# Down products of two feed-forwards: the middle eight inner tiles as 2x2 blocks with seven block products

## The reference, cut to what matters

```
x = x + (silu(hn @ w_up[:, :2816]) * (hn @ w_up[:, 2816:])) @ w_down                 # first block
u = causal_dwconv(h @ w_up, conv_w, 3 taps) + conv_b;  gate, val = split(u)           # second block
x = layer_norm(ALPHA * x + (1 + gt_f) * ((silu(gate) * val) @ w_down), g, b)
```

## Time and profile before

| | |
|---|---|
| median of 3 runs | 3579.56 us (3576.22 to 3579.78) |
| the profiled execution | 3572.89 us, span 3571.2 us |
| PE busy | 3412.1 us (96%), 16130 matmuls |
| DVE busy | 1965.6 us (55%) |
| ACT busy | 1356.3 us (38%) |
| POOL busy | 461.3 us (13%) |

### The profile page before, as it was taken

One profiled execution on the slowest core, in us unless ns is written; L12 is line 12 of the kernel. 1 busy time (PEld: TensorE's weight loads), 2 busy tenths in 40 slices (PEclk: granted clock), 3 DMA queues, 4 the chain that ended last, 5 costly groups with the idle time before them and its releaser, 6 DMA issues.

```text
span 3571.2 us, 39536 instructions
## 1 busy us (share of the span) xinstructions
PE 3412.1 (96%) x16130; PEld 2770.9 (78%) x16130; DVE 1965.6 (55%) x2371; ACT 1356.3 (38%) x1880; POOL 461.3 (13%) x325
## 2 busy tenths in 40 slices
PE   7999999999899899999999999999899989999998
PEld 4778887877777578888888877777698768888886
DVE  7454452233554434687773264444576678888335
ACT  3232112333145733433331146353545454444213
POOL 0000000000001000344540010000000035554000
PEclk9999999999999999999999999999999999999999
DMA  3213241112410013233238322120203312333732
GB/s 111 61 38 123 97 165 60 48 48 81 139 51 27 27 51 112 95 112 111 107 122 320 112 83 92 59 100 30 95 1 124 118 71 106 113 112 140 309 105 83
DMA packets 114390, 353.82 MB, mean 99 GB/s; under 512 B 16009, under 2 KB 25993, under 8 KB 114193
## 3 DMA queue, kind: packets, MB, share of 16 engines
q1 hardware_dynamic: 114208, 351.28, 28.1%
HBM read 268.15 MB, written 81.91 MB: 98 GB/s over the span
## 4 chain that ended last, share of the span: by engine, by line
PE 82%; DVE 8%; ACT 7%; issue 1%; DMA 1%; SPq 0%; ACTq 0%; DVEq 0%
PE PS L491 41%; PE PS L2334 21%; PE PS L474 8%; PE PS L3678 1%; PE PS L1817 1%; PE PS L3690 1%; PE PS L2809 1%; ACT whi L431 1%; DVE wlo L436 1%; PE PS L1526 1%; ACT dS L1580 1%; PE PS L503 1%; PE PS L918 1%; PE PS L1839 1%; PE PS L509 1%
## 5 line engine op out<-in xcount | busy, mean ns | idle before, releaser
L436 DVE TENSOR_TENSOR wlo<-raw,whi 128x1024 fp32r<-128x1024 f32 (+3 forms) x393 | 499.1, 1271 | 443.9 <-ACT whi L431 441.3
L431 ACT CAST whi<-raw 128x1024 fp32r<-128x1024 f32 (+3 forms) x393 | 372.4, 948 | 745.4 <-PE PS L491 337.1
L491 PE MATMUL PS<-xhi,whi 128*128 128x512 f32 x1904 | 617.6, 406 | 32.5 <-DVE xlo L525 12.8
L491 PE MATMUL PS<-xlo,whi 128*128 128x512 f32 x1904 | 594.7, 394 | 0.0
L491 PE MATMUL PS<-xhi,wlo 128*128 128x512 f32 x1904 | 592.2, 392 | 0.0
L491 PEld LDWEIGHTS PS<-xhi,whi 128*128 128x128 f32 x1904 | 355.3, 191 | 123.5 <-issue 28.6
L491 PEld LDWEIGHTS PS<-xlo,whi 128*128 128x128 f32 x1904 | 362.2, 190 | 78.0
L491 PEld LDWEIGHTS PS<-xhi,wlo 128*128 128x128 f32 x1904 | 361.5, 190 | 77.8
L2334 PE MATMUL PS<-tf,whi 128*128 128x512 f32 x936 | 288.2, 389 | 1.7 <-DVE wlo L436 1.7
L2334 PE MATMUL PS<-xhi,whi 128*128 128x512 f32 x624 | 243.8, 391 | 7.2 <-DVE xlo L2319 5.6
L2334 PE MATMUL PS<-xlo,whi 128*128 128x512 f32 x624 | 243.5, 390 | 0.0
(11 more groups left out here) (553 smaller groups left out, 5554.2 us busy)
## 6 DMA issues: line engine op xcount, KB each, us to landing
raw<-in_w_up SPq DMA_DIRECT2D x88, 512.0 KB, 3.4
hid<-hs SPq DMA_DIRECT2D x88, 512.0 KB, 3.6
raw<-in_w_in SPq DMA_DIRECT2D x67, 512.0 KB, 3.2
slot<-hid SPq DMA_DIRECT2D x56, 512.0 KB, 6.5
adr<-in_w_ada SPq DMA_DIRECT2D x48, 512.0 KB, 4.5
raw<-in_w_down SPq DMA_DIRECT2D x48, 512.0 KB, 3.5
raw<-in_w_gate SPq DMA_DIRECT2D x32, 512.0 KB, 3.3
merged<-hid SPq DMA_DIRECT2D x16, 512.0 KB, 12.8
```

The source lines that it names most:

```text
L431: act.e.copy(whis[i % RING][:, ks, :], raws[i % RING][:, ks, :]).then_inc(*give("w_hi", i))
L436: dve.e.tensor_tensor(wlos[i % RING][:, ks, :], raws[i % RING][:, ks, :], whis[i % RING][:, ks, :].bitcast(F32), ALU.subtract).then_inc(*g ...
L491: ins = pe.e.matmul(ps[:, h * 512:(h + 1) * 512], w[s][:, k, :], x[:, h * 512:(h + 1) * 512], start=(at == 0 and n == 0), stop=(at == kt - ...
```

## The change

The middle part (hidden tiles 6 to 13) of both feed-forwards is no longer eight products of 8 x 3 x 2 = 48 matmuls (384 in all). Output tiles j and j+4 together, inner tiles {6, 8, 10, 12} against {7, 9, 11, 13}, and the two halves of the tokens form a 2x2 block product with seven block products of 12 matmuls: 4 x 84 = 336 matmuls.

- Weights: the host reorders the inner tiles (`DOWN_ORDER`); POOL makes sums of the weight halves as in the up products; there are `_s12` and `_s34` units in the plan.
- Hidden tiles: four sums of block halves are made beside the up products. In the iteration behind tiles 6, 8, 10, 12 VectorE makes `h1` in place; behind tiles 7, 9, 11, 13 it makes `h2`, `h3` and `h4`, ScalarE casts them (`sums_hi`, `last_hi`) and VectorE makes their `lo` (`h23_lo` over 1024 tokens, `h4_lo` over 512). SP stores them too (`store_sums`).
- Down: seven operand forms (B11, B21, B22, T1 to T4) of 2 MB each are loaded from `hid`, in rows of 2 KB, in place of eight hidden tiles of 1 MB. ScalarE copies two of the seven results, and VectorE adds to the residual in 11 operations of 512 tokens for each j.
- The last part begins with three half products interleaved tile by tile, since hidden tiles 18 to 21 can only be loaded when the last forms are no longer read.

```diff
+        def down_blocks_pe(pe, f):
+            as_banks()
+            def part(unit, at, form, name, read, *signal):
+                pe.wait_ge(f"lane{FORM_LANE[form]}", f, "form", 1)
+                block_product(pe, unit, at, DF[form], (name, f, j), read, *signal)
+            for j in range(4):
...
+                part(a, 0, "B11", "d1", ("dn_p1", f, j), "dn_1", f, j)
+                part(a, 4, "B21", "d2", ("dn_c11", f, j), "prod", a)
+                part(b, 4, "T4", "d4", ("dn_c21", f, j), "prod", b)
+                part(s12, 0, "T1", "d5", ("dn_p5c", f, j), "dn_5", f, j)
+                part(s12, 4, "T2", "d6", ("dn_u2", f, j), "prod", s12)
+                part(s34, 0, "T3", "d7", ("dn_u3", f, j), "dn_7", f, j)
+                part(s34, 4, "B22", "d3", ("f%d_x" % f, 1, j), "prod", s34)
+            as_pairs()
...
+        def other_sums(dve, f, i, u, v):
+            n = SECOND[i]
+            dve.wait_ge(f"f{f}_lo", i - 1)
+            dve.wait_ge(f"f{f}_h", i)
+            dve.e.tensor_tensor(u[:, half[1]], v[:, half[1]], u[:, half[1]], ALU.subtract).then_inc(*give("h2", f, n))
+            dve.wait_ge("h2", f, n)
+            dve.e.tensor_tensor(u[:, half[0]], u[:, half[1]], u[:, half[0]], ALU.subtract).then_inc(*give("h3", f, n))
...
+            for j in range(4):
+                begin_sp(sp, DOWN[f], j, 6)
+                if j == 0:
+                    load_form(sp, f, "T3")
+                    load_form(sp, f, "B22")
+                    load_hidden(sp, f, 14)
+                    load_hidden(sp, f, 15)
...
-            for ft in range(8):
-                down_half(pe, 1, ft, 0, hs)
-            for ft in range(8):
-                down_half(pe, 1, ft, 1, hs)
+            drive([down_half(pe, 1, ft, 0, hs) for ft in range(3)])
+            for ft in range(3, 8):
+                drive([down_half(pe, 1, ft, 0, hs)])
+            for ft in range(8):
+                drive([down_half(pe, 1, ft, 1, hs)])
                 ln0_first_pe(pe, ft)
```

More of the change, by code:

```diff
@@ L142, in weight_plan @@
     ups("w_up", PLAIN[0])
[L143 to L147, removed]
+    downs("w_down")
     tiles("w_in2", [ft for _, ft in PROJ], 8)
@@ L151, in weight_plan @@
     ups("w_up2", PLAIN[1])
[L152 to L157, removed]
+    downs("w_down2")
     return plan
@@ L2269, in ffn_pool @@
+            for i in range(18, 22):
+                load_hidden(sp, f, i)
+            for ft in range(16):
+                begin_sp(sp, DOWN[f], ft % 8, 14)
         def ffn_pool(pool, f):
@@ L2323, in build, with block_product @@
         fast = [6, 7, 0, 1, 2, 3, 4, 5]
+        def block_product(pe, unit, at, x, name, read, *signal):
+            w, ps = unit % RING, bank.take(pe, fast, name, read)
+            pe.wait_ge("w_lo", unit)
+            for k in range(4):
+                for n, (ws, xs) in enumerate(((whis, x[0]), (whis, x[1]), (wlos, x[0]))):
+                    ins = pe.e.matmul(ps, ws[w][:, at + k, :], xs[:, k, :], start=(k == 0 and n == 0), stop=(k == 3 and n == 2))
+            ins.then_inc(*give(*signal))
         def seven_pe(pe, f, i):
@@ L2329, in part @@
             def part(unit, at, x, name, read, *signal):
-                w, ps = unit % RING, bank.take(pe, fast, (name, f, i), read)
-                pe.wait_ge("w_lo", unit)
-                for k in range(4):
-                    for n, (ws, xs) in enumerate(((whis, x[0]), (whis, x[1]), (wlos, x[0]))):
-                        ins = pe.e.matmul(ps, ws[w][:, at + k, :], xs[:, k, :], start=(k == 0 and n == 0), stop=(k == 3 and n == 2))
-                ins.then_inc(*give(*signal))
+                block_product(pe, unit, at, x, (name, f, i), read, *signal)
             part(a, 0, B11, "p1", ("sv_p1", f, i), "sv_1", f, i)
@@ new lines, in down_blocks_act @@
+        def down_blocks_act(act, f):
+            for j in range(4):
+                begin_act(act, DOWN[f], j, 6)
+                if j:
+                    act.wait_ge("dn_u2", f, j - 1)
+                else:
+                    act.wait_ge(f"f{f}_lo", 21)
+                act.wait_ge("dn_1", f, j)
+                act.e.copy(D1, bank.of(("d1", f, j))).then_inc(*give("dn_p1", f, j))
+                begin_act(act, DOWN[f], j + 4, 6)
+                begin_act(act, DOWN[f] + "_s12", j, 6)
+                if j:
+                    act.wait_ge(f"f{f}_x", 1, j - 1)
+                act.wait_ge("dn_5", f, j)
+                act.e.copy(D5, bank.of(("d5", f, j))).then_inc(*give("dn_p5c", f, j))
+                begin_act(act, DOWN[f] + "_s34", j, 6)
```

331 lines of the change are left out of this document (254 added, 77 removed).

## The result

The changed kernel takes 3594.86 us (median of 4 runs, 3594.17 to 3595.61), the kernel before 3577.89 us (4 runs, 3573.21 to 3579.78). The ratio is 1.0049 with a 95% interval of 1.0032 to 1.0067: slower by 17 us, where 3577.7 was forecast and 3588 was the upper end. The profiled execution took 3594.76 us, its span 3593.0, 21.8 more than before.

What follows compares the result with a forecast made beforehand. TensorE, running without a gap, was taken to bound the kernel. Gain -21.8, borders +10.5 and sums +9.4 gave -1.9 us: 3571.0 us profiled, 3577.7 us as median, range 3564 to 3588 us.

Steps and rivals of the forecast that it cites:

- the gain: Middle part: 336 matmuls in place of 384 save 10.9 us in each feed-forward, 21.8 us in all.
- the two bank waits at the first border: First to middle part: first block product waits for VectorE's addition to free its bank, 1.6 us in both feed-forwards.
- the second's last part: Second feed-forward's last part: waits of 1.4 us for the third and 1.4 us for the fourth half product.
- the loads of the forms: Middle part: T3 and B22 load after the first part but land before needed, hidden by block products; cost nothing.
- Rival A: Second feed-forward's up stage hides the sums, so they cost nothing there: -11.3, 3568.3 us; chance 0.28.
- The sum in the second up stage: VectorE's and POOL's SBUF needs added: 18.6 of 19.04 us taken, so added operations cost PE 9.4 us of waits.
- Sums beside the up products: Up blocks: added VectorE operations, 4.4 us a pair, cost 0 in the first feed-forward, 9.4 us in the second.
- the bound for "nothing may be late": Second up stage: upper bound of 13 us on the sums' cost if no delay goes unnoticed by PE.
- 4.6 us that were to be late unseen: Second up stage: a `lo` 3.4 us late plus one POOL operation of 1.15 us, taken off 14 us.
- the fourth half product's wait: First feed-forward's last part: fourth half product waits for its weights' `lo`, 2.6 us with start and restart.
- rival C: Middle part: 2 KB rows at half of 408 GB/s land forms late, 8.7 us each feed-forward; +15.5, 3595.1 us; chance 0.15.

Runs made afterwards that it cites:

- banks: Changed kernel with the turn of the eight PSUM banks set by hand at three places: 3591.22 us, ratio 1.0048 to the kernel before.
- free sums: Changed kernel with banks' turns set, last part opened 4, 2, 2 inner tiles at a time, sums, casts and stores left out: 3559.54 us, ratio 0.9954.
- thin with all repairs: Changed kernel with all four repairs, last part opened 4, 2, 2 inner tiles at a time, sums over 64 of 512 columns: 3565.26 us, ratio 0.9974.
- early stores: Changed kernel with the three stores of the sums ahead of the next weights' load on SyncE, not between two loads: 3586.66 us, ratio 1.0031.
- chunks of 4: Changed kernel with the last part's three opening half products taking four inner tiles each in turn, not one: 3598.80 us, ratio 1.0065.
- all four: Changed kernel with every repair: banks' turns set, stores early, weights' low part and U2 ahead of sums, opening by four tiles: 3580.78 us, ratio 1.0016.

## Why the prediction was wrong

Right: the gain (-10.8 and -10.4 us for -10.9 each), the two bank waits at the first border (+1.5 and +1.7 for 1.6), the second's last part (+2.9 for 2.8), and the loads of the forms (0.4 us for nothing). The last of these held by luck: the form came 1.8 us later than the sum had it, and the wait at the border before it is what covered that. Where the banks' turn takes that wait away, PE waits 0.6 to 0.8 us for a form in the first and 1.7 to 2.2 us in the second feed-forward (banks, free sums, and thin with all repairs). Rival A, that the second up stage hides the sums, is out: with every repair it costs 15.3 us. The sum in the second up stage from both engines' claims on SBUF was the right kind of sum, and the new waits for `wlo` there, 10.5 us, are near its 9.4. The rule of the Trainium skill that it named ("SBUF — State Buffer", "Who interferes with whom") held here for the convolution steps as well, 2.05 to 2.20 us beside POOL for 1.27 us alone.

The step that failed is "Sums beside the up products". It took 0 us for the first feed-forward (bounds 0 and 2) and 9.4 for the second (0 and 13); measured are 5.4 and 25.8. Its parts by the runs (they overlap: in the second they add up to 27.2 us, with the banks taken from one run and the others from other ones):

- *The turn of the banks, 6.1 us in the second, nearly all at its opening.* Not in the sum at all. The middle part's 28 bank takes turn a list that the next up stage uses. The prediction priced where the new products take banks, not where they leave the list. Shown by the banks run (-5.5) and by free sums (371.57 us).
- *The queue on SyncE, 5.4 us in the first and 5.8 us in the second.* The step counted the sums' VectorE operations and left their three stores out of the sum, though they stand between two weight loads that POOL needs. Shown by early stores in the first, where PE's waits are gone; in the second the same run gives the 5.8 us, of which 1.5 are waits and the rest fewer slow matmuls.
- *VectorE and POOL, 15.3 us in the second*, for which 9.4 stood in the sum with 13 as its bound. 11.7 us go with the columns. What the columns and the small steps cost lies 2.3 us over the term's upper bound. The sum itself, 3.5 us short in each pair, gives 14 us; the bound for "nothing may be late" was put at 13 all the same, and the term took off 4.6 us that were to be late unseen. Without that deduction it is within 1.3 us of what was measured. Why the deduction did not hold no run shows.

In the changed kernel these meet: PE waited 10.5 us for `wlo` behind the opening, and some 7 us more are matmuls at a low granted clock behind three of these waits (0.78, 0.50, 0.84, 0.51 in four stretches of 5 us). The same is true of the first's last part, where the fourth half product's wait was 2.4 us as forecast (2.6 with start and restart), and the 1.6 us missing are slow matmuls behind it (0.75). The forecast had no term for that.

Weighed wrongly, too: rival C, at +15.5 us, gave the right time (3595.1 for 3594.9 us) by luck: its reason, forms 8.7 us late in each feed-forward, did not happen. The turn of the banks, the queue and the sums, not the late forms, were the slow side.

## What to carry to other kernels

When new work takes turns from a shared list (banks, slots, queue places), follow the list to its next user, and let each stage begin with the same turn. When sums are added to an engine, count their stores too, by what stands behind them in the queue. An operation added to a stage in which VectorE and GpSimd both claim SBUF for 98% of the time is not hidden: with every repair 17.6 us of added operations cost PE 15.3 us. With the repairs the same change gained 7.5 us where VectorE had 20% free, and lost where it had 12%. And when a wait is taken away, look at what it covered: here a form that came late behind it.

## What the runs showed of the hardware

The granted clock fell behind some of PE's waits. After the wait of 3.54 us below it was 0.50 for 5 us, with matmuls 0.43 us apart where 0.227 is the 2.4 GHz level's distance, that is the 1.2 GHz level. Rows of the changed kernel around such a wait:

```profile
3142.37 0.39 PE L2407 MATMUL PS<-xhi,wlo 128*128 128x512 f32 x1
3146.30 0.77 PE L2407 MATMUL PS<-xhi,whi 128*128 128x512 f32 x1 [3.54 <-DVE wlo L442]
3146.86 0.63 PE L2407 MATMUL PS<-xlo,whi 128*128 128x512 f32 x1
3147.29 0.63 PE L2407 MATMUL PS<-xhi,wlo 128*128 128x512 f32 x1
```

The length of the single wait does not settle it. Behind the wait of 2.37 us in the first's last part the clock was 0.66 in the changed kernel (2051.5 to 2056.5 us) and 1.00 in the banks run (2051 to 2056). Behind 2.76 us (early stores, 3100 to 3105) and 3.13 us (chunks of 4, 3145 to 3150) it was 1.00; behind 1.88 us (all four, 3187 to 3192) it was 0.66, where two waits as long in the same run had 1.00 behind them. In the chunks run two waits of 1.1 and 1.6 us close together were followed by 0.61 [the window above], and in the first up stage of the changed kernel, with waits of 0.8 to 1.2 us some 10 us or more apart, it was 1.00.

By PE's rows, a wait of 2.7 to 3.6 us with slow matmuls behind it cost 5.2 to 6.6 us; without them, 2.76 us cost 3.0 and 3.13 us 3.4.
